# Two-layer block on one core: in the MLP's down phases X's banks are drained by ScalarE and added by DMAs, the second half gets a fourth seven-product step, and two weight sums become one operation

## What is computed

```python
# D_MODEL = 2048, D_FF = 8192, 256 tokens
h = rms_norm(x, norm_mlp_g[l])
x = x + jnp.square(jax.nn.relu(h @ w_mlp_up[l])) @ w_mlp_down[l]      # first block
...
u = rmsnorm(x, g_mlp) @ w_up
return x + jnp.square(jax.nn.relu(u)) @ w_down                        # second block
```

## Time and profile before

| what | us |
|---|---|
| median of 3 runs | 2652.0 (2650.37 to 2652.44) |
| the profiled execution, its own time | 2650.98 |
| its span, from the first to the last instruction | 2649.3 |
| PE busy | 2640.2, in 13478 matmuls |
| DVE busy | 1986.9 |
| ACT busy | 1366.9 |
| POOL busy | 30.3 |

### The profile page before, as it was taken

The page is one execution under the profiler, slowest core; times in us unless marked ns, Lnnn a source line. Parts: engine busy times, 40 slices in busy tenths (PEclk is TensorE's granted clock), DMA queues, the critical chain, the costliest instruction groups (busy, mean ns, idle before and its releaser), DMA issues.

```text
span 2649.3 us, 39598 instructions
## 1 busy us (share of the span) xinstructions
PE 2640.2 (100%) x13478; PEld 2233.5 (84%) x13478; DVE 1986.9 (75%) x2876; ACT 1366.9 (52%) x1865; POOL 30.3 (1%) x64
## 2 busy tenths in 40 slices
PE   9999999999999999999999999999999999999999
PEld 7888888888888888888888888888788888888887
DVE  6687876555555778798797567878787978879886
ACT  6455555444444554555554454456555555455453
POOL 0100000000000000000000000000000000000000
PEclk9999999999999999999999999999999999999999
DMA  7655556665655566556566555545555655655565
GB/s 277 236 175 182 190 173 197 204 201 194 203 191 188 177 199 205 187 196 198 190 206 210 190 176 175 173 150 191 171 175 190 199 198 192 205 190 196 187 205 175
DMA packets 141721, 511.06 MB, mean 193 GB/s; under 512 B 16134, under 2 KB 16439, under 8 KB 141464
## 3 DMA queue, kind: packets, MB, share of 16 engines
q1 hardware_dynamic: 136312, 493.86, 55.9%
q0 software_dynamic: 3840, 12.86, 1.5%
q10 hardware_dynamic: 1440, 2.62, 0.3%
HBM read 505.08 MB, written 4.21 MB: 192 GB/s over the span
## 4 chain that ended last, share of the span: by engine, by line
PE 96%; DVE 2%; ACT 1%; DMA 0%; issue 0%; SPq 0%; ACTq 0%; DVEq 0%
PE acc L1955 26%; PE acc L1952 13%; PE acc L1973 5%; PE acc L1991 4%; PE acc L1993 4%; PE acc L1992 4%; PE pS L1991 3%; PE pS L1993 3%; PE pT L1993 3%; PE pT L1991 3%; PE pS L1992 3%; PE pT L1992 3%; PE acc L1970 2%; PE pO L1991 2%; PE pO L1993 2%; PE pG L1993 2%
## 5 line engine op out<-in xcount | busy, mean ns | idle before, releaser
L1104 DVE TENSOR_TENSOR wlo<-raw,whi 128x1024 fp32r<-128x1024 f32 x938 | 1143.4, 1223 | 446.4 <-ACT whi L614 440.5
L614 ACT ACTIVATE whi<-raw 128x1024 fp32r<-128x1024 f32 x938 | 990.0, 1057 | 793.7 <-PE pT L1993 243.1
L1955 PE MATMUL acc<-a_w,whi 128*128 128x512 f32 x2944 | 935.8, 397 | 0.1
L1952 PEld LDWEIGHTS acc<-a_w,wlo 128*128 128x128 f32 x2944 | 553.2, 188 | 129.4
L1952 PE MATMUL acc<-a_w,wlo 128*128 128x256 f32 x2944 | 578.6, 278 | 0.0
L1955 PEld LDWEIGHTS acc<-a_w,whi 128*128 128x128 f32 x2944 | 451.5, 189 | 2.5 <-DVE a_w L1157 0.8
L1973 PE MATMUL acc<-a_w,whi 128*128 128x512 f32 x592 | 198.4, 404 | 0.0
L825 ACT ACTIVATE t<-acc 128x256 f32<-128x256 f32 x128 | 48.9, 382 | 170.0 <-PE acc L1955 169.9
L1970 PEld LDWEIGHTS acc<-a_w,wlo 128*128 128x128 f32 x592 | 111.4, 188 | 24.5
L1970 PE MATMUL acc<-a_w,wlo 128*128 128x256 f32 x592 | 116.8, 279 | 0.0
L1500 DVE TENSOR_TENSOR t<-acc,t 128x256 f32<-128x256 f32 x128 | 54.0, 422 | 74.9 <-ACT t L825 74.8
(11 more groups left out here) (496 smaller groups left out, 3962.8 us busy)
## 6 DMA issues: line engine op xcount, KB each, us to landing
raw<-stream SPq DMA_DIRECT2D x938, 512.0 KB, 3.4
gbias<-gateb POOLq DMA_DIRECT2D x12, 256.0 KB, 4.1
X<-x_rows POOLq DMA_DIRECT2D x4, 512.0 KB, 6.8
bias_scratch<-brow POOLq DMA_DIRECT2D x8, 256.0 KB, 5.5
q<-bias_scratch POOLq DMA_DIRECT2D x8, 256.0 KB, 3.8
out<-X ACTq DMA_DIRECT2D x8, 256.0 KB, 5.3
xF<-x SPq DMA_DIRECT2D x6, 256.0 KB, 6.8
bias<-bias_scratch POOLq DMA_DIRECT2D x8, 128.0 KB, 4.1
```

The source lines that it names most:

```text
L614: A(whi[:, slot, :], raw[:, slot, :], ACT.Copy).then_inc(s.hi_done, 1)
L1104: TT(wlo[:, slot, :], raw[:, slot, :], whi[:, slot, :].bitcast(F32), SUB).then_inc(s.lo_done, 1)
L1952: low = lambda: MM(ps[:, 0:T], wl, wide[:, k0 + k, 0:T], start=False, stop=False, skip_group_check=True)
L1955: last = MM(ps, wh, wide[:, k0 + k, :], start=start and k == 0, stop=not start and k == KC - 1, skip_group_check=True)
```

## The change

- Second half: the order of the row blocks becomes 4, 0, 5, 1, 6, 2, 3, 7, and block 3 becomes a seven-product step too. The first such step now stands second in the half; it stood third.
- X's four banks of a half in the six SECOND_GROUPS: ACT drains each bank with its scale into one of six tiles (drain_bank), and POOL issues a DMA that adds the tile to X in SBUF. DVE no longer touches X there. The adds of a layer are waited for by DVE in group 3 (drains_landed).
- The step banks: at g = 0 ACT copies them (drain_parts, at t = 0 of the second half, and at t = 14). At g = 1, 2 DVE adds them as before, those of the first half at t = 1 and 2, those of the second half now at t = 14 and 15.
- Two weight sums, d1 = b12 - b11 and b22 - b12, are one DVE operation of 2x512; sums lies ahead of raw in one buffer for that.
- WARM is 8, and the scratch for the descriptors of POOL's DMAs is set to 4096 bytes.

```diff
-WARM = 5
+WARM = 8
...
-BLOCK_ORDER = ((4, 0, 5, 1, 6, 2, 7, 3), (3, 4, 0, 5, 1, 2, 6, 7))
-BLOCK_STEPS = ((0, 1, 2, 3), (0, 1, 2))
+NDRAIN = 6
+DRAINS = 8 * 3
+BLOCK_ORDER = ((4, 0, 5, 1, 6, 2, 7, 3), (4, 0, 5, 1, 6, 2, 3, 7))
+BLOCK_STEPS = ((0, 1, 2, 3), (0, 1, 2, 3))
...
-        raw = sb("raw", NSLOT * CW)[0].rearrange("p (s c) -> p s c", s=NSLOT)
+        raw_f = sb("raw", 3 * COLS + NSLOT * CW)[0]
+        sums, raw = raw_f[:, 0:3 * COLS], raw_f[:, 3 * COLS:].rearrange("p (s c) -> p s c", s=NSLOT)
...
+            def add(dst):
+
+                k = added[0]
+                added[0] += 1
+                pool.dma_start(dst, drain[k % NDRAIN], accum_op=ALU.add).then_inc(drain_added[k % NDRAIN], 16)
+
+            def add_columns(i, n):
+
+                for h in range(2):
+                    pool.wait_ge(s.t_evac, 2 * (i + n) + h + 1)
+                    add(X[:, h, COLS * n:COLS * n + COLS])
...
+            def drain_bank(ps, scale, freed):
+
+                k = drained[0]
+                drained[0] += 1
+                if k >= NDRAIN:
+                    act.wait_ge(drain_added[k % NDRAIN], 16 * (k // NDRAIN))
+                A(drain[k % NDRAIN], ps, ACT.Copy, scale=scale).then_inc(freed, 1)
...
+            def drain_parts(layer, g, q):
+
+                r = phase(layer, g, q)
+                act.wait_ge(s.block_done, BLOCK_CHUNKS_AFTER[r])
+                if layer and not g:
+                    act.wait_ge(s.m_added, 8)
+                if r and not g:
+                    act.wait_ge(s.m_free, 4 * r)
+                for n in range(4):
+                    A(parts[q][n], (acc[0], acc[1], pV, pN)[n], ACT.Copy).then_inc(s.m_free, 1)
...
+                        def column(e, h):
+                            drain_bank(tbanks(At(i + e), True)[h], rsq[:, h:h + 1], s.t_evac)
+
+                        for t in range(16):
+                            if q and t == 0 and not g:
+                                drain_parts(layer, g, 0)
+                            if q and t == 14 and not g:
+                                drain_parts(layer, g, 1)
+                            if q and t >= 14:
+                                act.wait_ge(s.t_half, i + t - 13)
+                                column(t - 14, 0)
+                                act.wait_ge(s.mm_done, c + t + 1)
+                                column(t - 14, 1)
+                            if not q and t == 14:
+                                act.wait_ge(s.rb_ready, 4 if layer else 2)
+                                act.wait_ge(s.t_evac, 2 * i)
+                                act.wait_ge(s.t_half, i + 1)
+                                column(0, 0)
+                            if not q and t == 15:
+                                act.wait_ge(s.block_corner, p + 1)
+                                column(0, 1)
+                                act.wait_ge(s.t_half, i + 2)
+                                column(1, 0)
+                                column(1, 1)
+                            prep(At(c + t))
...
+                    if (layer, g) in SECOND_GROUPS:
+                        down_pair(0)
+                        down_pair(1)
+                    else:
+                        for n in range(NG):
+                            down(n, g == FF_GROUPS - 1)
...
-                TT(d1, b12, b11, SUB).then_inc(s.sums_step, 1)
-                dve.wait_ge(s.sums_step, 3 * k + 1)
+                both = lambda first, step: bass.AP(raw_f.tensor, first, [list(raw_f.ap[0]), [step, 2], [1, COLS]])
+                at = 3 * COLS + CW * slot
+                TT(both(0, at + CW), both(at + CW, COLS), both(at, CW), SUB).then_inc(s.sums_step, 1)
+                dve.wait_ge(s.sums_step, 2 * k + 1)
                 TT(d2, b22, d1, SUB).then_inc(s.sums_step, 1)
-                TT(b12, b22, b12, SUB).then_inc(s.sums_step, 1)
-                dve.wait_ge(s.sums_step, 3 * k + 3)
+                dve.wait_ge(s.sums_step, 2 * k + 2)
                 TT(d4, b21, d2, SUB).then_inc(s.sums_made, 1)
...
-                    if g:
-                        dve.wait_ge(s.m_free, 4 * phase(layer, g - 1, q) + 4)
-                    elif layer:
-                        dve.wait_ge(s.m_added, 8)
+                    dve.wait_ge(s.m_free, 4 * r)
                 for n in banks:
                     ps, part = (acc[0], acc[1], pV, pN)[n], parts[q][n]
-                    if g:
-                        TT(part, ps, part, ADD).then_inc(s.m_free, 1)
-                    else:
-                        V.tensor_copy(part, ps).then_inc(s.m_free, 1)
+                    TT(part, ps, part, ADD).then_inc(s.m_free, 1)
...
-                            if q and t in (1, 2):
+                            if q and g and t in (1, 2):
                                 part_sums(layer, g, 0, (0, 1) if t == 1 else (2, 3))
-                            if q and t in (12, 13):
-                                part_sums(layer, g, 1, (0, 1) if t == 12 else (2, 3))
-                            if q and t >= 14:
-                                n = 2 + t - 14
-                                for h in range(2):
-                                    xg = X[:, h, COLS * n:COLS * n + COLS]
-                                    evac_tok(At(c + t), At(i + t - 14), h, tbanks(At(i + t - 14), True),
-                                             lambda ps: STT(xg, ps, rsq[:, h:h + 1], xg, MUL, ADD))
-                            if not q and t == 14:
+                            if q and g and t in (14, 15):
+                                part_sums(layer, g, 1, (0, 1) if t == 14 else (2, 3))
+                            if (layer, g) not in SECOND_GROUPS and t == 14:
                                 dve.wait_ge(s.t_half, i + 1)
                                 corner(0, 0)
-                            if not q and t == 15:
+                            if (layer, g) not in SECOND_GROUPS and t == 15:
                                 dve.wait_ge(s.block_corner, p + 1)
                                 corner(0, 1)
                                 dve.wait_ge(s.t_half, i + 2)
...
+                        if ends and m == 1:
+                            drains_landed(dve, layer)
+                            dve.wait_ge(s.t_evac, done)
...
+    nc = bacc.Bacc("TRN2", target_bir_lowering=False, num_devices=1, dynamic_dma_scratch_size=4096)
```

More of the change, by code:

```diff
@@ L362, in program @@
         tsm = sb("tsm", 48)[0]
+        drain = [sb(f"drain{k}", COLS)[0] for k in range(3)]
         ssq = tsm[:, 0:16].rearrange("p (s h n) -> p s h n", s=2, h=2)
@@ L449, in program @@
         rg = take("rg", 8)[:, 0:4].rearrange("p (g h) -> p g h", h=2)
-        sums = sb("sums", 3 * COLS, F32, at=at_br)[0]
+        drain += [sb(f"drain{k}", COLS, F32, at=at_br + 4 * COLS * (k - 3))[0] for k in range(3, NDRAIN)]
         sums_hi = sb("sums_hi", 6 * COLS, F32R, at=at_br + 12 * COLS)[0].rearrange("p (k c) -> p k c", k=2)
@@ L478, in program @@
         wg_landed = [ctx.enter_context(nc.semaphore(f"wg_landed{k}")) for k in range(2)]
+        drain_added = [ctx.enter_context(nc.semaphore(f"drain_added{k}")) for k in range(NDRAIN)]
         gb_landed = [ctx.enter_context(nc.semaphore(f"gb_landed{k}")) for k in range(2)]
@@ L492, in phase, with drains_landed @@
             return BLOCK_PHASES.index((layer, g, q)) if (layer, g, q) in BLOCK_PHASES else None
+        def drains_landed(eng, layer):
+            for k in range(NDRAIN):
+                eng.wait_ge(drain_added[k], 16 * len(range(k, DRAINS * (layer + 1), NDRAIN)))
         def block_tile(p, m):
@@ L574, in _, with add_drains @@
                     pool.dma_start(gbias[n % 2], gateb[:, D * g + COLS * q:D * g + COLS * q + COLS]).then_inc(gb_landed[n % 2], 16)
+            added = [0]
+            def add(dst):
[6 more added lines that the diff above has]
+                    add(X[:, h, COLS * n:COLS * n + COLS])
+            def add_drains(layer, i0):
+                for g in range(FF_GROUPS - 1):
+                    i = i0 + 4 * g
+                    add_columns(i, 0)
+                    add_columns(i, 1)
+                    add_columns(i, 2)
+                    add_columns(i, 3)
+            add_drains(0, G_MLP1)
             pool.wait_ge(s.m_added, 8)
@@ L595, in _ @@
                     .then_inc(cumb_landed[m % 4], 16)
+            add_drains(1, G_MLP2)
         @block.scalar
@@ L807, in _ @@
                             mix_hi(At(3))
+            drained = [0]
+            def drain_bank(ps, scale, freed):
[13 more added lines that the diff above has]
+                    A(parts[q][n], (acc[0], acc[1], pV, pN)[n], ACT.Copy).then_inc(s.m_free, 1)
             def mlp(b, a, i0, layer, stage, gain, before):
@@ L833, in up, with down_pair @@
                             A(mixed_hi[:, m.base // 2, :], mixed, ACT.Copy).then_inc(s.mixed_hi, 1)
+                    def down_pair(q):
+                        c, i = b + 64 * g + 32 + 16 * q, i0 + 4 * g + 2 * q
```

(6 more changed lines are left out.)

1 line of the change is left out of this document (removed).

## The result

The changed kernel takes 2676.4 us (median of 6 runs, 2673.98 to 2679.16), the kernel before 2652.1 on the same chip (6 runs, 2650.37 to 2652.66): ratio 1.0093, 95% interval 1.0080 to 1.0106. It is slower by 24 us, the forecast was 16. Of the six runs of the kernel before two lie at 2650.4 and four at 2652.0 to 2652.7, while most of its runs beside the experiments lie at the lower level, so that a difference to the changed kernel, with both taken over the kernel before, is 1.2 to 1.5 us smaller than that of the plain medians.

What follows compares the result with a forecast made beforehand. TensorE was taken as the bound, busy 2640.2 of 2649.3 us. Four halves with new waits of 3.7 + 1.8 us, less 5.9 saved, gave +16 us on the median of 2652.0: 2668, range 2660 to 2681.

Steps and rivals of the forecast that it cites:

- the branch with the chance of 0.70: Whole kernel: the new waits come as reckoned, +11 to +22 us; chance 0.70.
- First step against the parts: Second half's first seven-product step, g = 1 and 2: TensorE waits 3.6 us for DVE's parts, in four halves.
- The half's end: Ahead of the next up phase, g = 1 and 2: TensorE waits 1.7 us for the last parts; nothing at g = 0.
- What is removed: Six second halves: 18 matmuls (4.1 us) and the old waits (1.8 us) go, together 5.9 us saved.
- The clock falls in the new pauses: Rival, four down phases: TensorE's clock drops after pauses of over 3 us, +11 us, 2679; chance 0.08.
- The adds delay the weights: Rival, 12 halves: the adding DMAs delay weight loads beyond the 4.5 us in hand, +32 to +65 us; chance 0.06.
- 4.5 us of delay are covered: Down phases: a weight load lands 3.4 us after issue, whi uses it at 1182.00, so the adds cost 0.
- The rest at nothing: X's 48 drains and adds, joined weight sum, WARM and smaller descriptor scratch: taken at 0 us.
- The step doesn't save: Rival, two adjoining steps: DVE's load stops TensorE and the third product's gain is lost, +4 us, 2672; chance 0.04.

Runs made afterwards that it cites:

- x1: Changed kernel, but at g = 1 and 2 VectorE adds all four step banks of the first half at that half's own t = 15: 2663.0 us.
- x5: Changed kernel with the second half's order 4, 5, 0, 1, 6, 2, 3, 7, so the first of four seven-product steps stands third: 2670.9 us.
- x2: Changed kernel, but at g = 1 and 2 all four step banks of the second half are added at t = 14: 2669.2 us.
- x4: Changed kernel, but at g = 1 and 2 the second half's first step does its first product six times, filling the pause with matmuls: 2669.8 us.
- x11b: x8 with WARM 5 again and the weight sums again four operations of 512 columns: 2645.3 us.
- x8: x3 without POOL's 48 adding DMAs, ScalarE's drains kept (X not the reference's): 2644.7 us.
- x6: x3, but POOL's 48 DMAs copy the drained tiles over X instead of adding them (X not the reference's): 2645.1 us.
- x3: Changed kernel with both the x1 and x2 edits, the step banks of both halves added earlier at g = 1 and 2: 2655.7 us.

## Why the prediction was right, and where it was not

The two new waits and the saving were right in size and in mechanism. That the total fell into 2660 to 2681 is in part luck: the branch with the chance of 0.70, +11 to +22, does not hold the measured +24, and the upper end of the range was made of longer waits for the parts, while what filled it were the clock and the late loads.

- *First step against the parts*: 3.6 us forecast, 3.47 measured, four times, none at g = 0. On the common clock the last part was put at 1186.0 and ended at 1186.40, where the half ran 0.55 us later. The chain drains, whi, sums_hi, sums_lo, wlo, parts is the one in the trace. x1 shows that the parts' place in VectorE's order decides, x5 that the step's earlier place makes the pause: with the step third, 0.4 us are left once the waits for late loads are taken off.
- *The half's end*: 1.7 forecast, 1.63 measured, by the chain named; x2 takes it away.
- *What is removed*: 5.9 forecast, 6.2 measured.
- *The clock falls in the new pauses*, a rival at 0.08 with +11: it happened, at half to two thirds of that (5.4 by x4, 7.5 in the profiled execution). The argument against it, that the array stood for 1.8 us ahead of the first chunk and went on at the higher pace, compared a pause with one half as long, and even that one lets the clock fall in some executions (x11b). The Trainium skill, "TensorE: Matmul & The Clock Gate", Part 1, was the better guide here: it says that idle time makes the array fall back to half its clock, and this trace agrees, with 0.53 behind 3.47 us, though in x2 one pause of that length left the clock at 1.00. The price was over-sized because it came from the start, 5.3 us of slow matmuls; behind a pause it is 3 to 5 us.
- *The adds delay the weights*, a rival at 0.06 with +32 to +65: the mechanism was right, the size not. The step that failed is "4.5 us of delay are covered". It counted up to whi at 1182.00, but the load it took, landed at 1174.1 + 3.4 = 1177.5, is read before that by the weight sum at 1178.95, so that only 1.4 us were covered; in x8 it is 0.1 to 1.2 us at the steps of the second halves but the last, which has some 3. The rest of the delay takes VectorE's reserve, of which 0.6 to 1.4 us are left at the adjoining step and which is slow to come back. Cost 5.9 in the changed kernel, partly hidden by its own pauses, 11.0 with these gone. The Trainium skill, "DMA: Bandwidth & Descriptors", "Issuing engines are not separate DMA queues", says that DMAs of all issuing engines share the same 16 engines and interleave; the delayed loads agree, and the copies of x6, under the same rule, cost 0.4.
- *The rest at nothing*: drains by ScalarE (x8) and WARM with the joined sum (x11b, within 0.6) hold.
- *The step doesn't save*, a rival at 0.04: at g = 0 it came true, for the reason above; x6 and x8 show that the step saves its three matmuls when the weights are on time.

The total was 8 us short, and both missing terms were listed as rivals and then priced singly, as if only one of them could happen.

## What to carry to other kernels

- Who empties a bank and who adds it up are two decisions. Let the engine that is early drain the bank into SBUF, since the matmuls wait for that alone, and put the addition into a stretch where the adding engine has idle time: here the same four steps cost 24 us or gain 5, by who adds and when.
- A saving in the matmuls' order moves when buffers must be free. Before moving a step forward, list what stands ahead of its releaser in that engine's queue, and what a pause of some us does to the clock behind it.
- Reckon reserve as a stock: what a double step draws from it, and what each pair pays back. And count a load's slack up to its first reader, here the weight sum, not up to one that reads it later: a delay of 3 us, under the 4.5 of whi, stopped the matmuls six chunks later.

## What the runs showed of the hardware

- DMAs that add 256 KB tiles within SBUF: a median of 7.5 us to landing with four close together, 4.3 one by one; plain copies 4.7 with four close together. GpSimd's issue of one takes 0.87 us against 0.54. Loads of 512 KB beside four of them land after 6.7 us (5.1 to 8.3) in x3, beside four copies after 4.1, and after 3.7 in x8.
- The clock fell behind pauses of 2.07, 2.24 and 3.47 us (granted clock 0.50 to 0.57 in the stretches that were read), and did not fall behind pauses of 1.63 to 1.93 us in the down phases; at the start it fell behind 1.94 us of idle time in one execution. Behind one of the four pauses of 3.47 us in x2 it did not fall (granted clock 1.00). Filling the pauses with useless matmuls made the kernel 5.4 us faster.
- Joining two weight sums saves next to nothing: the four operations took 2.66 us, the three take 2.59 (1206.11 to 1208.70 in x3).
